# Sample attention: sliding keys and new rows inside one quad's step, partial results added on VectorE, queries loaded once, steps written out

## What is computed

```python
def sample_attention(b):                       # for each of the 8 sequences
    # differential attention over 4096 cached keys and the 8 new ones
    s = q_d @ k_d.T * HD ** -0.5 - slope * dist
    p = softmax(s)                             # each component
    o_d = (p[:, 0] - lam * p[:, 1]) @ v_d
    # compressed branch: scores of 64-key blocks; their probabilities also choose 16 blocks
    o_c, chosen = compressed(q_n)
    # selected branch: the chosen blocks of the cache, and the new rows
    o_s = softmax(q_n @ k_sel.T * HD ** -0.5 - slope * dist, over=chosen) @ v_sel
    # sliding branch: the last 512 keys from a window buffer, and the new rows
    o_w = softmax(q_n @ k_win.T * HD ** -0.5 - slope * dist) @ v_win
    return gate[0] * o_c + gate[1] * o_s + gate[2] * o_w, o_d
```

## Time and profile before

| | us |
|---|---|
| median of 3 runs (4175.21 to 4187.73) | 4182.6 |
| profiled execution, its own time | 4168.58 |
| its span | 4167.1 |
| PE busy | 3539.4 (85% of the span) |
| DVE busy | 1572.0 (38%) |
| ACT busy | 1082.8 (26%) |
| POOL busy | 383.9 (9%) |
| mean granted TensorE clock | 0.927 of full speed |

### The profile page before, as it was taken

How to read it: one execution, slowest core, us unless ns; L and a number is a source line. 1 busy time by engine, 2 the same in 40 slices (tenths; PEclk the granted TensorE clock), 3 DMA queues, 4 the chain that set the end, 5 groups by cost and what they waited for, 6 DMA issues and landing times. The chain is left out here.

```text
span 4167.1 us, 65993 instructions
## 1 busy us (share of the span) xinstructions
PE 3539.4 (85%) x24514; PEld 3239.8 (78%) x24514; DVE 1572.0 (38%) x3298; ACT 1082.8 (26%) x2124; POOL 383.9 (9%) x507
## 2 busy tenths in 40 slices
PE   4999999956999829878888787999778499999995
PEld 3999999946999819856566555777678399999994
DVE  5332323262011013344454365556531633232325
ACT  2211221121111110034343354444322221122112
POOL 2000000012000003123332100000000300000001
PEclk7999999987999969989999888999889799999997
DMA  2111111103532266388878520000161111111111
GB/s 79 41 47 43 45 40 40 40 0 110 128 94 90 78 238 198 94 307 292 310 287 291 185 61 26 9 6 3 58 201 37 35 41 47 43 45 40 40 40 43
DMA packets 293890, 401.86 MB, mean 96 GB/s; under 512 B 50197, under 2 KB 222614, under 8 KB 293638
## 3 DMA queue, kind: packets, MB, share of 16 engines
q1 hardware_dynamic: 255654, 309.55, 23.1%
q0 software_dynamic: 24368, 79.26, 5.4%
q10 hardware_dynamic: 13680, 10.72, 0.8%
HBM read 356.17 MB, written 47.27 MB: 97 GB/s over the span
## 5 line engine op out<-in xcount | busy, mean ns | idle before, releaser
L423 PE MATMUL ps<-f_hh,f_wh 128*128 128x364 f32 x2112 | 696.4, 330 | 81.3 <-DVE f_wl L368 81.3
L423 PE MATMUL ps<-f_hl,f_wh 128*128 128x364 f32 x2112 | 696.1, 330 | 0.0
L423 PE MATMUL ps<-f_hh,f_wl 128*128 128x364 f32 x2112 | 696.0, 330 | 0.0
L423 PEld LDWEIGHTS ps<-f_hh,f_wh 128*128 128x128 f32 x2112 | 398.4, 189 | 83.0 <-issue 83.0
L423 PEld LDWEIGHTS ps<-f_hl,f_wh 128*128 128x128 f32 x2112 | 398.6, 189 | 0.0
L423 PEld LDWEIGHTS ps<-f_hh,f_wl 128*128 128x128 f32 x2112 | 398.6, 189 | 0.0
L573 PE MATMUL ps<-pj_hh,pj_wh 128*128 128x364 f32 (+1 forms) x936 | 308.8, 330 | 52.3 <-DVE pj_wl L558 52.3
L368 DVE TENSOR_TENSOR f_wl<-f_raw,f_wh 128x1024 fp32r<-128x1024 f32 x132 | 157.2, 1220 | 507.0 <-ACT f_wh L342 485.7
L443 PE MATMUL ps<-f_uh,f_wl 128*128 128x364 f32 x1056 | 348.1, 330 | 0.0
L443 PE MATMUL ps<-f_ul,f_wh 128*128 128x364 f32 x1056 | 346.1, 328 | 0.0
L443 PE MATMUL ps<-f_uh,f_wh 128*128 128x364 f32 x1056 | 345.5, 327 | 0.0
(11 more groups left out here) (361 smaller groups left out, 5698.1 us busy)
## 6 DMA issues: line engine op xcount, KB each, us to landing
dpage<-cache_diff_kv SPq DMA_DIRECT2D x256, 512.0 KB, 7.4
f_raw<-ffn_w SPq DMA_DIRECT2D x132, 512.0 KB, 4.2
npage<-cache_nsa_kv POOLq DMA_DIRECT2D x256, 128.0 KB, 5.8
z_scratch<-pj_z POOLq DMA_DIRECT2D x38, 546.0 KB
pj_raw<-w_in SPq DMA_DIRECT2D x38, 512.0 KB, 4.3
pages<-cache_nsa_kv SPq DMA_DIRECT2D x96, 128.0 KB, 3.4
pages<-cache_nsa_kv POOLq DMA_DIRECT2D x80, 128.0 KB, 4.8
pages<-cache_nsa_kv ACTq DMA_DIRECT2D x80, 128.0 KB, 5.1
```

What stands on the lines that cost most here:

```text
L423: last = pe.matmul(G.ps[:, s + c, 0:CH], w[a][:, j % 3, k * P:(k + 1) * P], h[b][:, k, c * CH:(c + 1) * CH], start=(k == 0 and n == 0), st ...
```

## The change

`sample_attend` is written anew. A sequence has eight steps, one a quad. The window's keys are a sixth key tile of the sixth quad's step (`WIDE = 5`), and its scores, those of the new rows, their exponentials, their transposes and their values are computed within that step, into free columns of banks 5, 6 and 7; in the two beats after it key tiles use banks 0 and 1 alone. `turn_probs` waits for the diff exponential before the four diff transposes and for the other before the last two. `fold` is cut in two: minima in the beat where a sequence ends, weights (`share`) two beats later. The partial outputs are multiplied by their weights and added up in SBUF by DVE, ten instructions in each of two beats (`add`, `add_rest`), the compressed branch included; then one product for each part adds up over partitions, in the beat of the next sequence's wide step's keys, and DVE copies the result out of bank 5. The exchange of the statistics goes into `turn_probs` as well. PE, ACT and DVE have all 64 steps written out; SP and POOL keep their loops. Queries and new keys of all sequences are loaded and scaled once, in `gates`; `sample_select` and `sample_attend` read them there.

The diff, cut to its core:

```diff
 def sample_select(nc, G):
-        q = sb("q", [P, NB, ROWS])
+        q = G.qn
-            pool.memset(q[:], 0.0).then_inc(q_cleared, 1)
-            sp.wait_ge(q_cleared, 1)
-            for h in range(KVH):
-                for g in range(GRP):
-                    sp.dma_start(q[h * HD:(h + 1) * HD, :, c:c + TS], ...).then_inc(q_in, 16)
-            dve.wait_ge(q_in, 16 * NSA_H)
-            then(dve.tensor_scalar(q[:], q[:], -HD ** -0.5, None, ALU.mult))
 def sample_attend(nc, G):
+    WIDE = 5
+    for x in KEYS:
+        banks = (0, 1) if x[0] > WIDE and x[0] % QUADS in (WIDE + 1, WIDE + 2) else (0, 1, 7)
+        turn += 1
+        KEY_BANK[x] = banks[turn % len(banks)]
         def _(sp):
             def small(g, j):
-                loads.append((qd[part, j, :, c * TS:(c + 1) * TS], ...))     # and qn, new_k: six loads
                 loads = [new_v (three), window]
             def round_(g, first, last):
                 ...
+                    if q == 4:
+                        small(g, 1)
+                    if q == 12 and not last:
+                        small(g + 1, 0)
         def _(pool):
+            pool.memset(new_v[:], 0.0).then_inc(cleared, 1)
+            pool.memset(newT[:], 0.0).then_inc(cleared, 1)
         def _(pe):
+            def scores(n):
                 ...
+                if is_wide(n):
+                    for half in range(2):
+                        for h in range(KVH):
+                            pe.matmul(G.ps[row:row + 32, 7, 0:HT], G.qn[...], kT[:, n % 2, 5, half * HT:(half + 1) * HT], ...)
+                            pe.matmul(G.ps[row:row + 32, 7, HT:HT + TS], G.qn[...], G.new_k[:, 4 + half, new], ...)
+                    for h in range(DIFF_H):
+                        mm = pe.matmul(G.ps[32 * h:32 * h + 32, 7, HT + TS:HT + 2 * TS], G.qd[:, s, h, :], G.new_k[:, h, new], ...)
+                mm.then_inc(sn_ready, 1)
+            def turn_probs(n, swap, join):
+                wait(pe, p_copied, n)
+                pe.wait_ge(exp_d, n + 1)
+                for a in range(QUAD):
+                    pe.transpose(G.ps[:, 4, a * P:(a + 1) * P], pd[:, n % 2, a * PAGE:(a + 1) * PAGE], G.ident[:])
+                pe.wait_ge(exp_n, n + 1)
                 ...
+                if join is not None:
+                    pe.wait_ge(added, (join + 1) * ADDS)
+                    pe.matmul(G.ps[:, 5, 2 * P:2 * P + 32], acc[:, 0:VD], G.comb_d[:], start=True, stop=True)
+                    mm = pe.matmul(G.ps[:, 5, 2 * P + 32:2 * P + 32 + ROWS], acc[:, VD:VD + KV1], G.comb_n[:], start=True, stop=True)
+            pe.wait_ge(cleared, 2)
+            for n in range(STEPS_ALL + 2):
+                scores(n - 1); values(n - 2); turn_keys(n); turn_probs(n - 1, ended(n, 0), ended(n, 5))
         def _(act):
+            def exps_n(n):
+                if is_wide(n):
+                    act.activation(pw[:], pw[:], ACT.Exp, ...)              # window, 256 wide
+                    act.activation(p_new[:, 0, :], p_new[:, 0, :], ACT.Exp, ...)   # new rows, 8 wide
+                    act.activation(p_new[:, 1, :], p_new[:, 1, :], ACT.Exp, ...)
+                act.activation(pn[:, n % 2, :], pn[:, n % 2, :], ACT.Exp, ...).then_inc(exp_n, 1)
         def _(dve):
+            def add(s, first, end):
+                for i in range(first, end):
+                    if i > 0:
+                        dve.wait_ge(added, base + 2 * i - 1)
                     ...
+                    dve.scalar_tensor_tensor(acc[:, 0:VD], o[:, j, i, 0:VD], w_d[:, i:i + 1], acc[:, 0:VD], ALU.mult, ALU.add).then_inc(added, 1)
+                    dve.wait_ge(added, base + 2 * i)
+                    dve.scalar_tensor_tensor(acc[:, VD:VD + KV1], o[:, j, i, VD:VD + KV1], own_n[:, k:k + 1], acc[:, VD:VD + KV1],
+                                             ALU.mult, ALU.add).then_inc(added, 1)
+            for n in range(STEPS_ALL + 5):
+                soft(n - 1); key_copies(odd tiles of n); copy_p(n - 1, ended(n, 0), ended(n, 5))
+                fold(ended(n, 0)); share(ended(n, 2)); add(ended(n, 3), 0, 5)
+                add(ended(n, 4), 5, QUADS + 1); add_rest(ended(n, 4))
 def gates(nc, G):
         def _(sp):
             sp.dma_start(raw[:], G.z[Z_NG, 0:N_GATE, 0:SEQ]).then_inc(raw_in, 16)
+            sp.dma_start(zd[:], ...).then_inc(queries_in, 16)                # and zn, two loads
+            sp.dma_start(G.new_k[:, 0:DIFF_H, :], ...).then_inc(keys_in, 16)  # and two more heads
             sample_gates(sp, 0)
             load_pages(nc, G, sp, mybir.EngineType.SP, 0, 0, 0)
         def _(pool):
+            pool.memset(G.qd[:], 0.0).then_inc(queries_cleared, 1)
+            pool.memset(G.qn[:], 0.0).then_inc(queries_cleared, 1)
         def _(dve):
+            dve.wait_ge(queries_in, 48)
+            for c in range(2):
+                dve.tensor_scalar(G.qd[...], zd[...], -HD ** -0.5, None, ALU.mult)
+                dve.tensor_scalar(G.qn[...], zn[...], -HD ** -0.5, None, ALU.mult)
```

More of the change, by code:

```diff
@@ L1217, in sample_attend @@
     rounds = NB // 2
[L1218 to L1222, removed]
+    N = 2 * QUADS
+    STEPS_ALL = NB * QUADS
+    WIDE = 5
+    HT = QT // 2
+    NN = QUADS + 2
     NSTAT = NN + 1
     N_SEL = QUADS + 1
[L1226 to L1260, removed]
@@ L1262, in before @@
-    def before(steps, n):
-        return sum(1 for m in steps if m < n)
-    def key_tiles(n):
[L1268 to L1277, removed]
@@ L1318, in small @@
             def small(g, j):
-                sp.wait_ge(cleared, 4)
-                wait(sp, tail[j], g * 2)
-                col = bass.ds(g * (2 * TS) + (ROW0 + j * TS), TS)
+                if not isinstance(g, int) or g > 0:
+                    sp.wait_ge(tail[j], g)
                 row = bass.ds(g * (2 * TS) + j * TS, TS)
[L1324 to L1333, removed]
@@ L1495, in values @@
                 for a in range(2):
                     for half in range(2):
-                        page = 2 * half + a
-                        v = npage[:, quad(n) % RING, page, 1, :] if is_page(n) else window[:, j, page, 1, :]
                         rows = slice(half * ROWS, (half + 1) * ROWS)
-                        last = pe.matmul(G.ps[rows, 6, VD:VD + KV1], pnT[:, n % 2, a * P + half * ROWS:a * P + (half + 1) * ROWS], v,
-                                         start=(a == 0), stop=(a == 1))
@@ L1522, in beat @@
[L1522 to L1525, removed]
-                if two:
-                    values(*two)
-                if now:
-                    turn_keys(*now)
-                for which in ended(g, n, 1):
-                    swap(*which)
-                if one:
-                    turn_probs(*one)
-                for which in ended(g, n, 4):
-                    join(*which, n >= N)
@@ L1537, in _ @@
-            all_beats(pe, beat)
-        def key_copies(eng, g, n, t, copied, copy):
-            m, _, _ = turned_before(n, t)
-            wait(eng, sn_ready, g * N + (n - 1))
-            eng.wait_ge(k_turned, g * ALL_T + m + 1)
-            copy(kT[:, n % 2, t, :], G.ps[:, KEY_BANKS[m % len(KEY_BANKS)], :]).then_inc(copied, 1)
-        def slot(n):
-            return quad(n) % QUADS if is_page(n) else QUADS + 1 if n % STEPS == S_WIN else QUADS
+                        mm = pe.matmul(G.ps[rows, 6, VD:VD + KV1], pnT[:, n % 2, 0, a * P + half * ROWS:a * P + (half + 1) * ROWS],
+                                       npage[:, r, 2 * half + a, 1, :], start=(a == 0), stop=(a == 1))
```

590 lines of the change are left out of this document (302 added, 288 removed).

## The result

The changed kernel takes 4077.8 us in the median of four runs (4071.4 to 4079.6), the kernel before 4178.9 (4172.3 to 4187.7). The ratio is 0.975 with a 95% interval of 0.973 to 0.978: faster, and 2 us from the forecast. The two profiled executions took 4168.6 and 4071.4, 97.2 apart. Between the stages' closing barriers in the two traces, the attention of the sample group went from 596.9 to 501.3 (-95.6), the selection from 30.2 to 26.4 (-3.8), the gates from 27.8 to 29.2 (+1.4); the rest is +0.8.

What follows compares the result with a forecast made beforehand. PE was taken as nearest its limit, in a chain with ACT and DVE. Attention -107, loads +5, queries at the front -7.8 and gates +3.4 gave -106.4: 4062 us by the profile, 4076 against the median, range 4045 to 4120.

Steps and rivals of the forecast that it cites:

- eight page beats: Sample attention: four diff transposes fit into PE's idling, a beat falls from 6.83 to 6.44 us, 51.5 a sequence.
- wide step: Sixth of eight steps, with window and new rows: 4.8 us a sequence, with its sixth transposed tile.
- scores of the new rows: Wide step: sixteen passes over eight columns on PE, between 0.2 us if overlapping and 1.0 if taking turns.
- three exponentials: Wide step, on ACT: one over 256 and two over 8, with nothing beside, 1.15 us a sequence.
- additions and share: DVE, two beats a sequence: twenty additions 0.29 us apart, and the weights, expose 1.9 us a sequence.
- join and swap: Two products instead of 40 passes, small copies, the swap and its two copies: 1.3 us a sequence.
- Loads: Page loads of the attention: between 0 and 2.5 us of waiting a sequence, taken as 0.6, 5 in all.
- The first rival: Loads become the bound, pages landing as late as 13.6 us, no beat under 7.8: 4096 us, chance 0.13.
- Begin and end: Attention: 6.1 us gained at the first queries; tail 22 us from the last step's keys, where it was 31.3.
- Selection: Front of selection: eight loads no longer issued or waited for, the stage's last transfer waits no longer, 7.8 us gained.
- Gates: Gates stage: five more loads on SP ahead of sample gates and page loads, 3.4 us lost.
- Rival 2: DVE becomes the bound: additions 0.39 us apart with POOL's masks in their way, 3.0 a sequence, 4100 us; chance 0.07.

Runs made afterwards that it cites:

- run 10: Kernel with five slots, with the wide step's products of the new rows' scores left out: 4047.9 us against 4046.0.
- run 9: Kernel with five slots, with the wide step's three extra exponentials done twice, first into a tile nobody reads: 4052.3 us.
- run 8: Kernel with five slots, with 18 of the 20 additions of every sequence left out: 4030.8 us.
- five slots: Changed kernel with five page slots and four quads ahead instead of four and three, SP and POOL rounds written out, `o_new` with one buffer: 4046.0 us.
- runs 1 and 3: Changed kernel with PE waiting for both exponentials again: 4078.1 us; the same with the window issued behind quad 7 instead of quad 4: 4074.1 us.
- run 6: Changed kernel with the rounds of SP and POOL written out instead of looped: 4070.3 us, ratio 0.975 to the kernel before.
- Run 5: Changed kernel with the selection issuing two quads ahead and the third issued at the begin of the attention: 4069.0 us.
- run 12: Kernel with five slots, with the window issued behind quad 7 and only two quads ahead in the selection: 4044.8 us, ratio 0.969.

## Why the prediction was right, step by step

The hit is luck in part. Two terms were wrong in opposite directions: in the 62 beats the chain was put 10 us too long and the waits for pages 19 too short. That only 2 us are left against the median is chance too, since by the profile it is 9. For one sequence, us:

| term | predicted | measured | where |
|---|---|---|---|
| eight page beats | 51.5 | 51.6 | 8 x 6.45 |
| wide step | 4.8 | 4.9 | first sequence, without additions: 7.62, 9.54, 7.10, each less 6.45 |
| of it, scores of the new rows | 0.67 | 0.16 | run 10 |
| of it, three exponentials | 1.15 | 0.6 | 1.05 less 0.44, rows of run 9 |
| additions and share | 1.9 | 0.83 | run 8 |
| join and swap | 1.3 | 0.15 | 7.71 - 7.62 (run 8) and 6.51 - 6.45 |
| the chain | 59.5 | 57.5 | median beats of five slots (447.9 in its 62 beats) |
| waits for pages, and POOL's standstill | 0.6 | 3.0 | (471.9 - 447.9) / 8 |

**Page beats: right.** 6.45, and runs 1 and 3 show that the split wait is the cause (6.83 without it).

**Wide step: right in the sum, not in its parts.** The new rows' passes were put too high, since they overlap, and so were the exponentials: "with nothing beside" is wrong for the 0.44 that lies beside the diff transposes, which the split wait lets go ahead. So the other pieces (turning, copies, values, two banks), 2.98 by the prediction, must take about 4.1. Which of them was not separated.

**Additions: put at more than twice their price.** They stand 0.26 apart (the median), not 0.29, and more of them lies beside PE than the 1.76 and 0.3 that I allowed for.

**Join and swap: too high.** The join's products run 0.3 to 0.4 us each and the copies behind them no longer:

```profile
1889.32 0.31 PE L1399 MATMUL ps<-c_comb_d,sa_acc 128*128 128x32 f32 x2
1889.46 0.41 PE L1400 MATMUL ps<-c_comb_n,sa_acc 128*128 128x64 f32 x2
...
1889.91 0.19 DVE L1546 COPY s_odT<-ps 128x32 f32<-128x32 f32 x1 [0.29 <-PE ps L1400]
```

To the next product, at 1889.80, it is 0.48, as foreseen (0.46). But in the first sequence, which has nothing to join, PE idles 0.24 at the same place and starts 0.10 behind the end of DVE's last key copy, so from its last transposes to the scores it takes 0.63 there and 0.70 with the join. I had counted every piece as exposed; by the beats 0.15 is.

**Loads: the step that failed.** "Between 0 and 2.5 us of waiting a sequence; I take 0.6" was argued from the mean rate, the landing of single pages (7.4 in the median, 13.6 at most) and a slot that is used again 12.9 before its keys. The window is 512 KB in SP's queue ahead of one quad, whose pages then land 12.2 to 15.0 us after the quad's first issue (11.2 behind the standstill). And they have less than 12.9: in the plain beats a quad is issued 11.3 before its keys (quad 3 of the second sequence: 1857.82 to 1869.11). I named the window's bytes and not its place. 24 us in the 62 beats against 5, and 3.2 a sequence in run 6, where there is no standstill, above the upper bound of 2.5. The first rival's mechanism, pages later than the two beats allow, did come, but not in every beat: in the changed kernel it is mainly one of eight, in run 6 two (9.10 from 4 to 5, 8.92 from 5 to 6).

The Trainium skill was weighed here by a figure of 358 GB/s for one core (DMA: Bandwidth & Descriptors, Specifications). The runs decide against it: 365 GB/s in the mean of 448 us, with every page early. The skill itself says so in another place (HBM Reference, Specifications (TRN2)): the figure is a core's share when both cores of a pair stream, and a core alone measures well above it. Here one core runs, and the rows agree with that sentence.

**Begin and end: right.** From the stage's start to the second quad 7.9, foreseen 9.0; the tail 21.5, foreseen 22. At the begin 2 us of it are the clock of this one execution: a first beat of 5.89 at a granted 0.76, where most of the experiments have 7.93 at 0.50.

**Selection: 3.8 instead of 7.8.** The step "the stage's last transfer doesn't wait longer" failed. The first product came 8.3 earlier in the stage's time, but the diff pages were issued 6.0 earlier (1769.59 less 1761.8 before, 1765.42 less 1763.6 after) and were in only 3.5 earlier; in both kernels the copy of `drop` lands within 0.5 of the last of the three quads. So it waits 9.6 instead of 5.2. Why the pages, issued 6.0 earlier, were in only 3.5 earlier was not separated. Run 5 shows that fewer loads ahead of the copy take the wait away, and run 12 that this can be lost again on quad 2's pages.

**Gates: +1.4 instead of +3.4.** Not looked into.

Altogether, in the profiled runs: for the 62 beats the chain was put at 458 and takes 447.9, 10 too long; the waits were put 19 too low, the selection 4; gates, begin and tail 4 too high. Some 9 us remain, by which the profiled run is above 4062.

## What to carry to other kernels

When a tuned stage gets shorter, price the loads by each transfer's place in its queue and by how long its slot is free before it is asked for, not by the mean rate: one large transfer ahead of a quad cost more here than all the additions. Price a part of a change on a version in which nothing else can absorb it; undone alone, the split wait and the additions both looked nearly free, and were worth some 20 and 13 us. A sum that comes out right says little of its terms.

## What was not expected of the hardware

Rival 2 named a mechanism that is real, though rare. An addition that meets POOL's mask ends behind it. With five slots:

```profile
1996.87 0.34 DVE L1609 SCALAR_TENSOR_TENSOR sa_acc<-sa_o,sa_own_n,sa_acc 128x128 f32<-128x128 f32 x1
...
1997.40 1.17 DVE L1609 SCALAR_TENSOR_TENSOR sa_acc<-sa_o,sa_own_n,sa_acc 128x128 f32<-128x128 f32 x1
1997.78 0.63 POOL L1319 TENSOR_TENSOR sa_masked<-c_bias_n,drop 128x256 f32<-128x256 f32 x1
...
1998.09 2.06 PE L1351 MATMUL ps<-ident,dpage 128*128 128x128 f32 x16
...
2007.04 1.09 PE L1351 MATMUL ps<-ident,dpage 128*128 128x128 f32 x8
```

The addition takes 1.17 instead of 0.34 and ends 0.16 behind the mask; the beat (1998.09 to 2007.04) is 8.95 instead of 8.13. In the changed kernel the first scaling of a sequence meets a mask in six of the eight, its twin behind it never (shortest, median, longest in ns):

```profile
L1601 DVE TENSOR_SCALAR sa_acc<-sa_o,sa_w_d x8: 278/683/996, 1873.6 to 2283.9; 128x128 f32<-128x128 f32 x8
```

```profile
L1602 DVE TENSOR_SCALAR sa_acc<-sa_o,sa_own_n x8: 274/277/282, 1874.4 to 2284.1; 128x128 f32<-128x128 f32 x8
```

Of the 160 additions and scalings of the changed kernel each one above 0.5 us overlaps a mask in time, and none that overlaps one ends before it. The Trainium skill (SBUF — State Buffer, Terms) says that Vector and GpSimd share a pair of ports of which only one holds the lock for a whole instruction; the rows agree that one waits for the other, for operations with one input tile in SBUF as well as with two. The wait shows on Vector's side alone, also where, as here, the addition's recorded start is 0.38 ahead of the mask's: no mask takes longer than 0.63. Whether POOL waits ahead of a mask's recorded start, the rows don't show. Only eight of the 160 overlap a mask, and six of these are above 0.5, so the price stays far below the 3.0 a sequence of rival 2.
